# Thirteen expert groups beside routing and gates instead of fourteen, eighteen groups of half-size products instead of seventeen, and a look-up of key numbers in four sets of slots

## The reference, cut to what matters

```python
def peer_ffn(x, w_query, sub_keys, u_tab, v_tab):
    def one_block(xc):
        q = (xc @ w_query).reshape(-1, PEER_HEADS, 2, PEER_HALF)
        s1 = jnp.einsum('thd,hkd->thk', q[:, :, 0], sub_keys[:, 0]).astype(jnp.float32)
        s2 = jnp.einsum('thd,hkd->thk', q[:, :, 1], sub_keys[:, 1]).astype(jnp.float32)
        v1, i1 = lax.top_k(s1, PEER_TOPK)
        v2, i2 = lax.top_k(s2, PEER_TOPK)
        cand = (v1[..., :, None] + v2[..., None, :]).reshape(*v1.shape[:-1], PEER_TOPK * PEER_TOPK)
        cidx = (i1[..., :, None] * PEER_N_KEYS + i2[..., None, :]).reshape(*i1.shape[:-1], PEER_TOPK * PEER_TOPK)
        sv, pos = lax.top_k(cand, PEER_TOPK)
        eidx = jnp.take_along_axis(cidx, pos, axis=-1)
        gate = jax.nn.softmax(sv, axis=-1)
        u = u_tab[eidx]
        act = jax.nn.gelu(jnp.einsum('thkd,td->thk', u, xc), approximate=False)
        w = gate.astype(act.dtype) * act
        vv = v_tab[eidx]
        return jnp.einsum('thk,thkd->td', w, vv)
```

## Time and profile before

| | |
|---|---|
| median of 3 runs | 3692.99 us (3692.48 to 3694.72) |
| profiled execution | 3693.2 us, its span 3691.4 us |
| PE busy | 3646.9 us, 99% |
| PE weight loads | 3004.1 us, 81% |
| DVE busy | 2554.4 us, 69% |
| POOL busy | 2553.0 us, 69% |
| ACT busy | 1263.4 us, 34% |
| granted clock of PE | 0.999 |

### The profile page before, as it was taken

The page is one execution under the profiler, slowest core; times in us unless marked ns, Lnnn a source line. Parts: engine busy times, 40 slices in busy tenths (PEclk is TensorE's granted clock), DMA queues, the critical chain, the costliest instruction groups (busy, mean ns, idle before and its releaser), DMA issues.

```text
span 3691.4 us, 54301 instructions
## 1 busy us (share of the span) xinstructions
PE 3646.9 (99%) x18216; PEld 3004.1 (81%) x18216; DVE 2554.4 (69%) x4735; ACT 1263.4 (34%) x1851; POOL 2553.0 (69%) x1130
## 2 busy tenths in 40 slices
PE   8999999999999999999999999999999999999998
PEld 7778888888888888888887788888888888888886
DVE  7645979966665656677675469799656565657776
ACT  1651134454344434211126412344444344441110
POOL 6445553349999989877764555533599999998775
PEclk9999999999999999999999999999999999999999
DMA  4122247883333333445321223388634333434542
GB/s 155 69 69 103 104 143 219 248 247 120 125 133 140 114 125 135 184 185 190 137 105 69 80 99 108 137 242 250 213 127 149 122 114 127 149 121 183 204 182 103
DMA packets 221243, 537.87 MB, mean 146 GB/s; under 512 B 9408, under 2 KB 140736, under 8 KB 172864
## 3 DMA queue, kind: packets, MB, share of 16 engines
q1 hardware_dynamic: 47968, 337.14, 25.2%
q10 hardware_dynamic: 173152, 199.13, 16.4%
HBM read 437.67 MB, written 98.57 MB: 145 GB/s over the span
## 4 chain that ended last, share of the span: by engine, by line
PE 95%; DVE 2%; POOL 2%; issue 1%; ACT 0%; DMA 0%; DVEq 0%; SPq 0%; POOLq 0%; ACTq 0%
PE bank L1576 30%; PE bank L1577 29%; PE bank L1578 29%; PE bank L1905 2%; PE bank L1906 2%; POOL part_l L529 1%; PE bank L1702 1%; PE bank L1865 1%; PE bank L1690 1%; PE bank L1681 0%; PE bank L1682 0%; POOL part_h L541 0%; DMA landing<-stream 0%; DVE bank L1038 0%; PE bank L1654 0%
## 5 line engine op out<-in xcount | busy, mean ns | idle before, releaser
L529 POOL TENSOR_TENSOR part_l<-landing,part_h 128x1024 fp32r<-128x1024 f32 x496 | 1285.5, 2597 | 504.5 <-ACT part_h L790 420.9
L1576 PE MATMUL bank<-XTh,part_h 128*128 128x512 f32 (+1 forms) x2688 | 1047.5, 390 | 3.8 <-DVE XTl L1058 2.4
L1578 PE MATMUL bank<-XTh,part_l 128*128 128x512 f32 (+1 forms) x2688 | 1034.0, 385 | 0.0
L1577 PE MATMUL bank<-XTl,part_h 128*128 128x512 f32 (+1 forms) x2688 | 1034.0, 385 | 0.0
L541 POOL TENSOR_SCALAR part_h<-landing 128x1024 fp32r<-128x1024 f32 x252 | 323.6, 1284 | 514.5 <-PE bank L1578 392.8
L575 POOL TENSOR_TENSOR part_l<-vraw,part_h 128x1024 fp32r<-128x1024 f32 x238 | 595.8, 2526 | 68.3 <-ACT part_h L916 68.3
L1576 PEld LDWEIGHTS bank<-XTh,part_h 128*128 128x128 f32 x2688 | 505.2, 188 | 102.7 <-DVE XTl L1058 3.4
L1578 PEld LDWEIGHTS bank<-XTh,part_l 128*128 128x128 f32 x2688 | 505.1, 188 | 101.6
L1577 PEld LDWEIGHTS bank<-XTl,part_h 128*128 128x128 f32 x2688 | 505.7, 188 | 95.6
L1485 DVE TENSOR_TENSOR X<-X,bank 128x512 f32<-128x512 f32 x544 | 345.3, 681 | 87.0 <-PE bank L1578 87.0
L916 ACT CAST part_h<-vraw 128x1024 fp32r<-128x1024 f32 x238 | 242.2, 1045 | 340.9 <-POOL vraw L582 280.7
(11 more groups left out here) (221 smaller groups left out, 6156.6 us busy)
## 6 DMA issues: line engine op xcount, KB each, us to landing
landing<-stream SPq DMA_DIRECT2D x248, 1024.0 KB, 4.8
vraw<-stream SPq DMA_DIRECT2D x68, 1024.0 KB, 6.5
dense_gates<-spill ACTq DMA_DIRECT2D x32, 2048.0 KB, 9.2
gate<-dense_gates ACTq DMA_DIRECT2D x62, 1024.0 KB, 4.8
early_acts<-early ACTq DMA_DIRECT2D x112, 256.0 KB, 2.2
acts_in<-early_acts ACTq DMA_DIRECT2D x28, 1024.0 KB, 7.5
LNP<-ln ACTq DMA_DIRECT2D x4, 1024.0 KB, 4.9
X<-x SPq DMA_DIRECT2D x4, 512.0 KB, 7.6
```

The lines of the kernel that those rows point to most:

```text
L529: nc.gpsimd.tensor_tensor(halves(part_l[s], h), halves(landing[s], h), halves(part_h[s], h).bitcast(F32), ALU.subtract).then_inc(split.sem, 1)
L1576: nc.tensor.matmul(dst, sth, mvh, start=first, stop=False)
L1577: nc.tensor.matmul(dst, sth, mvl, start=False, stop=False)
L1578: return nc.tensor.matmul(dst, stl, mvh, start=False, stop=last)
```

## The change

Three things are changed together.

1. `EG` goes from 14 to 13 and `E_BEFORE` from 12 to 10: two early pieces fewer beside the routing, as many as before beside the gates. `SG` follows, from 17 to 18 groups with half-size products. One plain downward product (96 matmuls) goes with the early group.
2. `SG` is even now, so one such group is written out ahead of the loop (with buffers 1), and the loop runs 8 times over two groups as before. The number of plain downward groups is odd now, so one stands behind their loop, and the last product reads `Wh[0]` instead of `Wh[1]`.
3. The look-up is done in four sets of slots: set r holds the picks 4r to 4r + 3 of each head, and compares with, multiplies and sums only the first 4(r + 1) ranks. The ranks are first written in that order, with eight conversions of 128 columns instead of two of 512.

```diff
-EG = 14
-E_BEFORE = 12
+EG = 13
+E_BEFORE = 10
 E_WITHIN = 2 * EG - E_BEFORE
...
-                with act.Fori(0, SG // 2) as m:
+                seven_group(0, 1, False)
+                with act.Fori(0, SG // 2 - 1) as m:
                     for par in range(2):
-                        seven_group(2 * m + par, par, False)
+                        seven_group(2 * m + (par + 1), par, False)
                 seven_group(SG - 1, 0, True)
...
-                ch.mark(nc.vector.tensor_scalar(paf[:, :, 0, :], pab[:, 0, :, :], -1.0, None, ALU.add))
-                ch.link(nc.vector.tensor_copy(paf[:, :, 1, :], pab[:, 1, :, :]))
+                by_slot = paf[:].rearrange("p t f x -> p t (f x)").rearrange(
+                    "p t (r f h s) -> p t f h r s", r=TOPK // 4, f=2, h=RH)
+                for f in range(2):
+                    for tb in range(TB):
+                        of = pab[:, f, tb, :].rearrange("p (h r s) -> p h r s", h=RH, r=TOPK // 4)
+                        ch.mark(nc.vector.tensor_scalar(by_slot[:, tb, f], of, -1.0 if f == 0 else 0.0, None, ALU.add))
+                ch.wait()
 
                 for tb in range(TB):
-                    at = paf[:, tb].rearrange("p f (n t) -> p (f n) t", t=2)
-                    ch.link(nc.vector.tensor_tensor(
-                        pick[:], at.unsqueeze(2).broadcast_to([P, RH * TOPK, TOPK, 2]),
-                        iota2[:, 0:TOPK, :].unsqueeze(1).broadcast_to([P, RH * TOPK, TOPK, 2]), ALU.is_equal))
-                    by_head = pick[:].rearrange("p (h n) a t -> p h n (a t)", n=TOPK // 2)
-                    ch.link(nc.vector.tensor_tensor(
-                        by_head, by_head, kf2[:, tb].rearrange("p f h a t -> p (f h) (a t)").unsqueeze(2).broadcast_to(
-                            [P, 2 * RH, TOPK // 2, 2 * TOPK]), ALU.mult))
-                    ch.link(nc.vector.tensor_reduce(route[:, tb, 0:2, :].rearrange("p f (n t) -> p (f n) t", t=2),
-                                                    pick[:].rearrange("p m a t -> p m t a"), AX_X, ALU.add))
+                    by_rank = paf[:, tb].rearrange("p f x -> p (f x)").rearrange("p (r m t) -> p r m t", r=TOPK // 4, t=2)
+                    to_slot = route[:, tb, 0:2, :].rearrange("p f x -> p (f x)").rearrange(
+                        "p (g r n t) -> p r g n t", r=TOPK // 4, n=2, t=2)
+                    flat = pick[:].rearrange("p m a t -> p (m a t)")
+                    for r in range(TOPK // 4):
+                        wide = 4 * (r + 1)
+                        one = flat[:, 0:4 * RH * wide * 2].rearrange("p (m a t) -> p m a t", a=wide, t=2)
+                        ch.link(nc.vector.tensor_tensor(
+                            one, by_rank[:, r].unsqueeze(2).broadcast_to([P, 4 * RH, wide, 2]),
+                            iota2[:, 0:wide, :].unsqueeze(1).broadcast_to([P, 4 * RH, wide, 2]), ALU.is_equal))
+                        by_head = one.rearrange("p (g n) a t -> p g n (a t)", n=2)
+                        ch.link(nc.vector.tensor_tensor(
+                            by_head, by_head, kf2[:, tb].rearrange("p f h a t -> p (f h) (a t)")[:, :, 0:2 * wide].unsqueeze(
+                                2).broadcast_to([P, 2 * RH, 2, 2 * wide]), ALU.mult))
+                        ch.link(nc.vector.tensor_reduce(to_slot[:, r], one.rearrange("p (g n) a t -> p g n t a", n=2),
+                                                        AX_X, ALU.add))
...
-                with pe.Fori(0, SG // 2) as m:
+                seven_group(0, 1)
+                with pe.Fori(0, SG // 2 - 1) as m:
                     for par in range(2):
-                        seven_group(2 * m + par, par)
+                        seven_group(2 * m + (par + 1), par)
                 seven_group(SG - 1, 0)
                 down_group(0, end_h, end_l, [(seven_added.sem, seven_added.at(l, 7 * SG - 1 + n)) for n in range(2)])
                 down_group(1, Wh[0], Wl[0])
                 with pe.Fori(1, EG // 2) as m:
                     for par in (1, 0):
                         down_group(2 * m + (1 - par), Wh[par], Wl[par])
+                down_group(EG - 1, Wh[1], Wl[1])
```

More of the change, by code:

```diff
@@ L59 @@
 V_LAST = NP - 2
-assert P_UV + 4 * (NG - EG) == V_LAST and EG % 2 == 0 and NP % 2 == 0
+assert P_UV + 4 * (NG - EG) == V_LAST and EG % 2 == 1 and NP % 2 == 0
 SG = NG - EG - 1
@@ L75 @@
 NS = S_LAST + 2
-assert SG % 2 == 1 and NS == NP - 2 * SG and A_FIRST + A_PIECES == S_FIRST
+assert SG % 2 == 0 and NS == NP - 2 * SG and A_FIRST + A_PIECES == S_FIRST
 P1, P2, P3, P5, P4, P7, P6 = range(7)
@@ L334, in build @@
         spilled = [tally(f"spilled{i}", 16, 16 * S // 64) for i in range(2)]
-        gate_in = [tally(f"gate_in{i}", 0, 16 * n) for i, n in enumerate((NG - EG + EG // 2, EG // 2))]
+        gate_in = [tally(f"gate_in{i}", 0, 16 * n) for i, n in enumerate((NG - EG + EG - EG // 2, EG // 2))]
         w_split = tally("w_split", 0, TB)
@@ L340, in build @@
         early_saved = [tally(f"early_saved{i}", 0, 16 * EG) for i in range(4)]
-        acts_back = [tally(f"acts_back{i}", 0, 16 * EG // 2) for i in range(2)]
+        acts_back = [tally(f"acts_back{i}", 0, 16 * ((EG + 1 - i) // 2)) for i in range(2)]
         u_first = tally("u_first", 0, 2 * (NG - EG))
@@ L981, in _ @@
                     scale_rows((2 * p, 2 * p + 1))
-                    raw_highs(0, 0, p)
-                    sum_highs(0, p)
+                    raw_highs(0, 1, p)
+                    sum_highs(1, p)
                 for k in range(2):
@@ L998, in _ @@
                         down_highs(2 * m + par, par, (used.sem, used.at(l, 4 * m + (S_DOWN + 2 * par))), 2 * m + (par + 1))
-                for par in range(2):
-                    down_highs(EG - 2 + par, par, (used.sem, used.at(l, S_DOWN + 2 * (EG - 2 + par))), None)
+                for q in range(EG - 3, EG):
+                    down_highs(q, q % 2, (used.sem, used.at(l, S_DOWN + 2 * q)), q + 1 if q == EG - 3 else None)
                 root(root_in.at(l, 5), slice(0, 2))
@@ L1536, in _ @@
                 for p in range(2):
-                    gate_cross(0, 0, p)
+                    gate_cross(0, 1, p)
                     gate_chunk(0, 2 * p + 1)
-                    sums(0, 0, p)
-                    raw_lows(0, 0, p)
+                    sums(0, 1, p)
+                    raw_lows(0, 1, p)
                     if p == 0:
-                        sum_lows(0, 0, p)
+                        sum_lows(0, 1, p)
                         for k in range(2):
@@ L1545, in _ @@
                         nc.vector.memset(acc[:], 0.0).then_inc(acc_zero.sem, 1)
-                with dve.Fori(0, SG // 2) as m:
+                seven_group(0, 1, False)
+                with dve.Fori(0, SG // 2 - 1) as m:
                     for par in range(2):
-                        seven_group(2 * m + par, par, False)
+                        seven_group(2 * m + (par + 1), par, False)
                 seven_group(SG - 1, 0, True)
@@ L1555, in _ @@
                         dve_group(2 * m + par, par, (used.sem, used.at(l, 4 * m + (S_DOWN + 2 * par))))
+                dve_group(EG - 1, 0, (used.sem, used.at(l, S_DOWN + 2 * (EG - 1))))
                 dve.wait_ge(y_added.sem, y_added.at(l, 4 * (NG - SG - 1)))
```

2 lines of the change are left out of this document (1 added, 1 removed).

## The result

The changed kernel takes 3708.68 us (median of 6 runs, 3707.08 to 3709.85) beside 3693.09 us for the kernel before on the same chip (6 runs, 3692.48 to 3695.21). The ratio is 1.0041, with an interval of 1.0031 to 1.0051: 15.6 us slower, inside the predicted range and 6.5 us above the forecast of 3702.2.

The account below looks back on a forecast made before the run. PE, busy 99% of the span, was taken to bound the kernel. Two layers of -2.55 for groups and +7.15 for the wait give +9.2 us, 3702.4 profiled and 3702.2 as median, 0.25% slower; range 3695 to 3712 (0.79).

Parts of the forecast that it names:

- the slack of 13.8 us: At the transposes of the routes, DVE ended their inputs 13.8 us before PE came; the change spends this by removing 21.76 us.
- The groups, -2.55 us a layer: On PE, one more half-size group costs 40.97 us and the dropped pieces and downward product save 43.52: net -2.55 a layer.
- The look-up's walk: DVE and POOL stepped through by turns: each block costs 10.9 us, and the look-up ends at 529.2, only 1.8 us earlier.
- POOL's pair sets the end: At the scaling, POOL's pair of 528.28 runs until 533.05; look-up ends from 527.1 to 529.6 give losses of 7.1 to 7.4.
- the first block's scaling comes through between POOL's two: On DVE, the first scaling gets through at 530.8, the second waits for 533.05; PE transposes block one at 530.9.
- The wait, 7.15 us a layer: At PE's transposes of the routes, the last end at 534.2 instead of 527.05: a loss of 7.15 us a layer.
- The clock: Rival: PE's clock falls in the wait for routing, 1.6 to 2 us lost until full speed, 3706 us; chance 0.22.
- From the gates on, everything as before: Sign expected in the new profile: from the gates on, everything as before at its own distances.
- the case that I held likeliest, 3701 to 3703.5: The whole kernel's time with the forecast as it stands, 3702.2 us; chance 0.42.
- The look-up that comes through before POOL's pair: Rival: look-up ends before 527.0, PE waits only 1.6 us a layer, 3691.1 us; chance 0.14.
- The longer look-up: Rival: fixed costs over 0.23 us an operation cost another stall, look-up end 532.5 to 536, 3704 to 3712 us; chance 0.15.
- the slow access: Bound: four-dimensional access makes comparisons and products run at 1.04 ns a column, look-up end 548, 3735 us; no chance of its own.

Follow-up runs that it names:

- Experiment 1: The changed kernel with the old look-up, three instructions of 4096 columns a block instead of twelve: 3708.57 us, ratio 1.0043.
- experiment 4: The changed kernel with 20 and 8 useless matmuls on PE ahead of the first two blocks' transposes: 3702.70 us, ratio 1.0026.
- experiment 5: The changed kernel with ACT's high part of the last early piece moved behind the copies of the routes: 3703.57 us, ratio 1.0028.
- experiment 6: The changed kernel with the scaling done between the look-ups of first and second block, each block let go after its look-up: 3703.52 us, ratio 1.0028.
- experiment 3: The changed kernel with the look-up left out, ranks copied in its place, so experts are picked wrongly: 3688.25 us, ratio 0.9988.
- experiment 7: The changed kernel with four comparisons, then four products, then four sums a block, scaling between first and second block: 3690.72 us, ratio 0.9994.
- experiment 8: The changed kernel with sixteen comparisons, then sixteen products, then sixteen sums over all blocks, a `pick` buffer for each block: 3689.53 us, ratio 0.9991.

## Why the prediction was right, and what it missed

- **What bounds it, and the slack of 13.8 us**: right. The groups alone cost nothing on PE's side, and taking 21.76 us of pieces away made PE wait.
- **The groups, -2.55 us a layer**: right, -2.6 and -2.5. The eighteenth group costs 40.8 and 40.9 us.
- **The look-up's walk**: right, with all four blocks. It gave ends at 496.7, 507.5, 518.4 and 529.2; measured were 496.2, 507.0, 518.0 and 528.75, all of them 0.4 to 0.5 us earlier as the whole program is. The price is per POOL operation, as read from the earlier trace rows.
- **POOL's pair sets the end**: right. Experiment 1 shows it: a look-up that ends 1.7 us later gives the same time. One detail hung on 0.01 us: "the first block's scaling comes through between POOL's two" held in layer two and not in layer one, where the scaling was asked for that much too late and all twelve transposes had to wait.
- **The wait, 7.15 us a layer**: right, 7.3 where nothing else disturbs it (experiment 4).
- **The clock**: here the choice failed. I gave the fall 0.22, since the waits seemed "a shade shorter, with work between" than the 4.9 us of the earlier trace rows. It fell in both layers, in the changed kernel and in experiments 1, 5 and 6. The price was right: 2.0 us a layer beside 2 forecast. The comparison was not. In layer one there was no work between, but one stand of 7.24 us; in layer two the clock fell before the three transposes, so they could not have held it. And one fall at 4.9 us was no measure: in these eight waits the clock fell 2.2 to 5.0 us after PE's last matmul.
- **"From the gates on, everything as before"**: wrong by a small term. The first gates come back from memory 1.1 to 1.4 us later and eat a slack of 0.6 us; that is 0.6 and 0.3 us in the two layers of the changed kernel, 0.8 us in layer one of experiment 4 and nothing in its layer two, some 0.9 in both layers of experiment 3. The slack was in the trace of before, and I hadn't read it.
- **The turn of the layers**: +1.5 us in the profile of the changed kernel, with a granted clock of 0.66 there, not foreseen; why the clock falls there in some profiles is not explained.

The sum of the misses: clock 4.0, turn 1.55, gates 0.9, waits 0.2, the three transposes of layer one 0.2, less 0.5 of a shorter start and 0.1 of the groups, make 6.25; the profiled execution took 3708.58 us beside a forecast of 3702.4 for it, 6.2. So the time lies in the stated range because the range took in the rival with the clock (3706); the case that I held likeliest, 3701 to 3703.5, did not come.

The rivals: the look-up that comes through before POOL's pair did not happen, and experiments 7 and 8 show that this side exists (3690.7 and 3689.5) and one way to reach it. The longer look-up and the slow access did not happen in the changed kernel: a comparison of 1024 columns takes 0.69 us, the sum 1.22.

## What to carry to other kernels

Work that is taken away ahead of a wait is a saving only up to the slack that the wait has; read that slack first, and then who else holds what the late engine needs, since a short instruction that meets another engine's long one pays for the long one's rest. Where PE is made to wait for microseconds, count the clock too: here a wait of 1.4 us left it whole (experiment 7), and in one of 7.3 us it fell and made it cost 9.3. A long chain of short linked instructions is shortened more by issuing all of one kind in a row (28.9 us instead of 44.4 from first comparison to last sum, experiment 8) than by taking over a third of its columns away (44.4 instead of 46.6), but then look at what the engine held up owes to others. Here PE did not need all of that, and the best kernel lies 0.1% below the one before.

## What the runs showed of the hardware that was not expected

- Between linked instructions DVE and POOL take turns. Through a row of sixteen products in which none waits for the one before POOL did not get in: they took 6.51 us, and four POOL operations 15.96 us instead of 9.6 (experiment 8). Between comparisons in such a row it did (experiment 7, 6.12 us for four instead of 1.7).
- 0.09 us of lateness cost 2.1 us (experiment 6, 527.97 against 527.88), and 0.01 us as much (changed kernel, layer one, 530.07 against 530.06).
- From PE's last matmul to the fall of the clock it was 2.2 us at the shortest (experiment 5, layer one) and 5.0 at the longest (the same kernel, layer two).
- The clock fell to half at the turn of the layers in some profiles (window of 1870, 0.66) and not in others, between the same instructions.
- The fetch of 896 KB of gates took 14.3 us in the kernel before and 15.4 and 15.7 us with the new groups, at the same place of the program.
